# The sample's selection mask: four DMA copies on ScalarE's queue in place of two 32-row matmuls

## The chip, the cores and the metric

The kernel runs on one core of a Trainium2 chip. The metric is the device time of one execution in microseconds (us). The kernel before takes 2543.24 us, the median of three runs (2542.43 to 2546.84). TensorE is PE in the profile, VectorE is DVE, ScalarE is ACT, GpSimd is POOL, and SyncE is SP.

## What is computed

Two transformer layers run over 288 tokens: 256 prompt tokens and 32 sample tokens, which continue a stream with 512 cached positions. Each layer has one input projection, two kinds of attention side by side, an output projection and a squared-ReLU MLP (width 2048, inner width 8192), all in fp32. The part that the change touches is attention A of layer 0, in which an indexer scores every key and each query attends to its best ones only:

```python
score = jnp.einsum('bth,bths->bts', iwb.astype(F32), dots)
_, idx = lax.top_k(score, n_sel)
logits = jnp.einsum('btgrd,btkgd->btgrk', qg, k_sel) * scale
logits = jnp.where(valid[:, :, None, None, :], logits + bias, NEG_INF)
probs = jax.nn.softmax(logits, axis=-1)
```

For the 32 sample queries there are L = 544 keys (512 cached, 32 new), and 136 of them are kept per query. The kernel does not gather: it adds a mask, 0 for a chosen key and -1e30 for the others, to the bias and so to the logits.

## The kernel before

**The weight stream.** Nearly all the time goes into projections. The weights come as chunks of 128x1024 fp32, four to a group of output columns. SP loads each chunk into one of four `raw` buffers. ACT rounds it to fp32r (`high`, L839), DVE subtracts to get the remainder (`low`, L1201), and PE multiplies both halves in 24 matmuls of 288 columns (L405 to L407 in the phase here). The tiles `w_high` and `w_low` have two buffers each. So ACT's `high` of chunk c + 2 waits until PE is done with chunk c, DVE's `low` waits for that `high`, and PE's chunk c + 2 waits for that `low`.

**The windows.** Attention is cut in small pieces and laid between the chunks. Window w is the gap after chunk w of the phase on PE, and each of ACT and DVE has its own list of pieces for window w, beside the `high` or `low` of chunk w + 2. Each engine runs its list strictly in order. Attention A runs in `phase_beside`, next to the 48 chunks of B's input projection. Its 8 prompt jobs (one per head) start in windows 23 to 30. The two sample jobs, n = 8 and n = 9 (four heads each), start in windows 43 and 45. A sample tile has 128 partitions: four groups of 32, one for each head, and each group holds the 32 queries.

**The mask.** DVE finds the sample queries' top keys in rounds and breaks ties (`pick_ties`) in windows 39 to 41. The result is a tile of ones and zeros on 32 partitions, `score_s` (32x544), and DVE signals `A_chosen`. In window 42 (`W_SPREAD`) PE copies these 32 rows into all four partition groups by a product with a 32x128 matrix of stacked identities, `rep` (L696, L697). DVE turns ones and zeros in PSUM into 0 and -1e30 (L1590) and writes them to `sel_s` (128x544, SBUF). Then POOL adds `sel_s` to the bias tile of job 8 and of job 9 (L1797), each signalling `A_addend`.

**The sample job behind it.** In window 43 PE makes the scores of job 8 (L573, L574); DVE waits for `A_addend`, adds it (L1416) and takes the row maximum (L1424). In window 44 ACT takes the exponential (L965), DVE normalizes (L1434, L1440), and PE transposes the probabilities (`turn`, L590, L591). Before its `high` of window 42, ACT has stored a norm in DRAM (L925), and after it ACT issues a DMA that spreads that norm over 128 partitions (`spread_norm`, L933, into `proj`).

The lines around the mask:

```python
W_TIES_S = W_PICK_S[-1] + 1      # 39
W_SPREAD = W_TIES_S + 3          # 42
```

Of the kernel before, what the change touches and what calls it, by code (L numbers as in the profile page):

```python
# [7 lines left out]
ALU = mybir.AluOpType  # L8
# [6 lines left out]
P = 128  # L15
D = 2048
KT = D // P
TP, TS = 256, 32
T = TP + TS
L = 512 + TS  # L20
PAST = 512
H = 8
# [7 lines left out]
NEG = -1e30  # L30
# [71 lines left out]
W_SPREAD = W_TIES_S + 3  # L102
# [35 lines left out]
def build(nc, ins, outs):  # L138
    with ExitStack() as ctx:
        def sb(name, shape, dt=F32):  # L140
            return ctx.enter_context(nc.sbuf_tensor(name, shape, dt))
# [3 lines left out]
        def sem(name):  # L145
            if name not in sems:
                sems[name] = ctx.enter_context(nc.semaphore(name))
            return sems[name]
# [23 lines left out]
        ident = sb("ident", [P, P])  # L172
        ones = sb("ones", [P, P])
        fold = sb("fold", [P, TS])
        rep = sb("rep", [TS, P])
        gains = sb("gains", [P, 4, KT])
        qk_gain = sb("qk_gain", [P, 6])
        fbias = sb("fbias", [P, 1])
# [17 lines left out]
        flat = ps[:, :, :].rearrange("p b n -> p (b n)")  # L196
# [29 lines left out]
        def s3(at, a, b):  # L226
            return scr[:, at:at + a * b].rearrange("p (a b) -> p a b", a=a)
# [39 lines left out]
        score_s, work_s, equal_s = scr[0:TS, 7808:8352], scr[0:TS, 8352:8896], scr[0:TS, 7168:7168 + L]  # L267
        sel, sel_s = s3(8896, 2, TP), scr[:, 9408:9408 + L]
# [33 lines left out]
        squared, hid_high_ready, hid_low_ready = sem("squared"), sem("hid_high_ready"), sem("hid_low_ready")  # L302
# [3 lines left out]
        low_sums, summed = sem("low_sums"), sem("summed")  # L306
        consts = sem("consts")
        const_set = sem("const_set")
        NCONST = 5


        hid_at = {"A": 0, "B": JOBS, "mlp0": 2 * JOBS, "C": 2 * JOBS + 32, "D": 3 * JOBS + 32, "mlp1": 4 * JOBS + 32}
# [35 lines left out]
        def _(pe):  # L348
# [185 lines left out]
            def prelude(ph, w):  # L534
                for h in v_heads_at(ph, w):
                    turn_v(ph, h)
                for q in quads_at(ph, w):
                    norm_sums(*q)
# [148 lines left out]
                                         relu[u][:, L // 4 * c:L // 4 * (c + 1)], start=u == 0, stop=u == 1)  # L687
                last.then_inc(sem("A_scores_s"), 1)

            def spread():  # L690

                pe.wait_ge(sem("A_chosen"), 1)
                pe.wait_ge(sem("A_pt_copied"), H)
                pe.wait_ge(hid_low_ready, hid_at["A"] + H)
                pe.wait_ge(sem("B_v_copied"), H)
                pe.matmul(flat[:, 3072:3072 + PAST], rep[:, :], score_s[:, 0:PAST], start=True, stop=True)  # L696
                pe.matmul(flat[:, 3072 + PAST:3072 + L], rep[:, :], score_s[:, PAST:L], start=True, stop=True)\  # L697
                  .then_inc(sem("A_spread"), 1)

            def window_a(w):  # L700
                attend("A", w)
                prelude("A", w)
                early("B", w)
                if w == 0:
                    turn_iw()
                if w == W_DOTS_S:
                    sample_dots()
                if w == W_FOLD:
                    fold_heads()
                if W_DOTS <= w < W_DOTS + 8:  # L710
                    dots(w - W_DOTS)
                if w == W_LF + 2:
                    turn_cum()
                if w == W_SPREAD:
                    spread()

            def window_b(w):
                prelude("B", w)
# [94 lines left out]
            group(G_SMALL, G_SMALL % 2, X, tiles=1, rows=SMALL, apart=True)  # L813
            pe.wait_ge(consts, 16 * NCONST)
            phase_beside(G_INB, 0, window_a, WINDOWS["A"])
# [11 lines left out]
        def _(act):  # L827
# [115 lines left out]
            def prelude(ph, w):  # L943
                for q in quads_at(ph, w, -1):
                    squares(*q)
                for q in quads_at(ph, w, 1):
                    spread_norm(*q)
                for h in v_heads_at(ph, w):
                    copy_v(ph, h)
                for q in quads_at(ph, w):  # L950
                    rsqrt(*q)
# [93 lines left out]

            def window_a(w):
                prelude("A", w)
                if W_DOTS <= w < W_DOTS + 8:
                    dots_relu(w - W_DOTS)
                if W_DOTS_S <= w < W_DOTS_S + 2:  # L1050
                    sample_relu(w - W_DOTS_S)
                if w == W_LF - 1:
                    forget()
                attend("A", w)
                early("B", w)
# [92 lines left out]
            low_copy(2, 0)  # L1148
            act.dma_start(ident[:, :], ins["c_ident"]).then_inc(consts, 16)
            act.dma_start(fold[:, :], ins["c_fold"]).then_inc(consts, 16)  # L1150
            act.dma_start(rep[:, :], ins["c_rep"]).then_inc(consts, 16)
            act.dma_start(qk_gain[:, :], ins["qk_gain"]).then_inc(consts, 16)
            act.dma_start(fbias[ROWS, :], ins["fbias"]).then_inc(consts, 16)
            for n in range(3, IN_A):
# [33 lines left out]
        def _(dve):  # L1188
# [355 lines left out]
            def window_a(w):  # L1544
                prelude("A", w)
                if w == 0:
                    copy_iw()
                if W_DOTS_S <= w < W_DOTS_S + 2:
                    weigh_sample(w - W_DOTS_S)
                if w == W_FOLD:  # L1550
                    dve.wait_ge(sem("A_scores_s"), 1)
                    for c in range(4):
                        last = dve.tensor_copy(score_s[:, L // 4 * c:L // 4 * (c + 1)], ps[32 * c:32 * c + 32, 6, 0:L // 4])
                    last.then_inc(sem("A_score_copied"), 1)
                    dve.wait_ge(sem("A_score_copied"), 1)
                if W_DOTS <= w < W_DOTS + 8:
                    weigh_dots(w - W_DOTS)
                if w == W_LF - 1:
                    add_fbias()
                if w == W_LF:  # L1560
                    log_forget()
                if w == W_LF + 1:
                    run_cum()
                if w == W_LF + 2:
                    copy_cum()
                attend("A", w)
                if W_PICK <= w < W_TIES:
                    for i in range(2):
                        pick_round(i, score[:, i, :], work[:, i, :], P, w - W_PICK, ROUNDS_P)
                if W_TIES <= w < W_TIES + 2:  # L1570
                    i = w - W_TIES
                    chosen = sel[:, 1 - i, :]
                    for step in range(3):
                        ins_ = pick_ties(i, score[:, i, :], work[:, i, :], chosen, relu[1][:, 0:TP], P, TOP_P,
                                         chosen, step)
                    link(ins_)

                    dve.tensor_scalar(chosen, chosen, -1.0, -NEG, ALU.add, ALU.mult)\
                       .then_inc(sem("A_sel_p"), 1)
                for r in range(ROUNDS_S):  # L1580
                    if W_PICK_S[r] == w:
                        pick_round(2, score_s, work_s, TS, r, ROUNDS_S)
                if W_TIES_S <= w < W_TIES_S + 3:
                    ins_ = pick_ties(2, score_s, work_s, sel_s[0:TS, :], equal_s, TS, TOP_S, score_s,
                                     w - W_TIES_S)
                    if ins_ is not None:
                        ins_.then_inc(sem("A_chosen"), 1)
                if w == W_SPREAD:
                    dve.wait_ge(sem("A_spread"), 1)
                    dve.tensor_scalar(sel_s, flat[:, 3072:3072 + L], -1.0, -NEG, ALU.add, ALU.mult)\  # L1590
                       .then_inc(sem("A_sel_s"), 1)

            def window_b(w):
                attend("B", w)
# [112 lines left out]
            dve.wait_ge(sem("A_ik_set"), 1)  # L1707
            dve.wait_ge(consts, 16 * NCONST)

# [36 lines left out]
        def _(pool):  # L1746
            chain = [0]

            def link(ins_):
                chain[0] += 1  # L1750
                ins_.then_inc(sem("pool_chain"), 1)
                pool.wait_ge(sem("pool_chain"), chain[0])
# [29 lines left out]
            def masked(ph, n):  # L1782
                pool.wait_ge(sem(f"{ph}_bias{n % 2}"), 16 * (n // 2 + 1) + (48 if ph == "B" and n >= H else 0))
                a = addend[n % 2][:, 0:WIDE] if n < H else addend[n % 2][:, 0:L]
                if ph == "A":
                    m = sel.rearrange("p i s -> p (i s)")[:, 0:WIDE] if n < H else sel_s
                    if n == 0:
                        pool.wait_ge(sem("A_sel_p"), 2)
                    if n == H:
                        pool.wait_ge(sem("A_sel_s"), 1)  # L1790
                else:
                    if n == 0:
                        pool.wait_ge(sem("B_masks"), 32)
                    m = mask_b if n < H else mask_bs
                if ph == "B":
                    a, m = (a[:, P:WIDE], m[:, P:WIDE]) if n < H else (a[:, PAST:L], m)
                pool.tensor_tensor(a, a, m, ALU.add).then_inc(sem(ph + "_addend"), 1)  # L1797
# [244 lines left out]
```

## Time and profile before

| | us |
|---|---|
| median of three runs | 2543.24 |
| lowest and highest run | 2542.43, 2546.84 |
| the profiled execution | 2542.57 |
| its span | 2540.8 |
| PE busy | 2525.8 (99% of the span) |
| DVE busy | 1391.2 (55%) |
| ACT busy | 1006.8 (40%) |
| POOL busy | 62.7 (2%) |

A busy share counts the time in which an instruction runs on the engine. For PE the share is high because matmuls are pipelined and each lasts longer than the step to the next one; so the steps between starts tell more than durations. Times in the timeline are us from the span's start.

### The profile page before, as it was taken

How to read it: one execution, taken by the hardware profiler on the slowest of the kernel's cores; microseconds unless marked ns; L12 is line 12 of the kernel's file. 1: busy time of each engine (PE TensorE's matmuls, PEld its weight loads, DVE VectorE, ACT ScalarE, POOL GpSimd, SP SyncE). 2: the span in 40 equal slices, each digit the busy share in tenths (PEclk: the TensorE clock that was granted, in tenths of full speed). 3: DMA queues.
4: the chain of work that ended last, by engine and by line, in shares of the span. 5: the costliest groups of instructions: out<-in, count | busy, mean ns of one | idle time of the engine just before them, and what ended most of it. 6: DMA issues, size and time to landing. Idle time of an engine off the chain costs nothing.

```text
span 2540.8 us, 46922 instructions
## 1 busy us (share of the span) xinstructions
PE 2525.8 (99%) x19222; PEld 2492.8 (98%) x19222; DVE 1391.2 (55%) x1646; ACT 1006.8 (40%) x1277; POOL 62.7 (2%) x104
## 2 busy tenths in 40 slices
PE   9999999999999999999999999999999999999999
PEld 9989999999999999999999999999999999999999
DVE  5588776554554454455544564666545544544544
ACT  5344445333333333334433444454333333333332
POOL 0002120000000000000000000000000000000000
PEclk9999999999999999999999999999999999999999
DMA  6545555444444444444444545554444444444454
GB/s 232 182 163 174 197 201 206 164 166 165 166 167 166 166 165 166 167 166 165 162 166 167 180 164 201 199 180 161 166 166 166 166 166 166 166 166 166 166 180 148
DMA packets 118673, 439.20 MB, mean 173 GB/s; under 512 B 14194, under 2 KB 14452, under 8 KB 116180
## 3 DMA queue, kind: packets, MB, share of 16 engines
q1 hardware_dynamic: 109584, 398.47, 45.4%
q0 software_dynamic: 6304, 30.98, 3.4%
q10 hardware_dynamic: 2596, 6.97, 0.8%
q8 instruction: 151, 2.47, 0.4%
q14 instruction: 38, 0.31, 0.0%
HBM read 426.10 MB, written 10.19 MB: 172 GB/s over the span
## 4 chain that ended last, share of the span: by engine, by line
PE 96%; DVE 2%; ACT 1%; issue 1%; DMA 0%; POOL 0%; ACTq 0%; DVEq 0%; POOLq 0%
PE ps L405 28%; PE ps L407 28%; PE ps L406 28%; PE ps L372 2%; PE ps L374 2%; PE ps L373 2%; DVE w_low L1201 1%; PE ps L607 1%; ACT w_high L839 0%; PE ps L559 0%; PE ps L433 0%; PE ps L435 0%; PE ps L434 0%; DMA resid<-in_x 0%; PE ps L608 0%
## 5 line engine op out<-in xcount | busy, mean ns | idle before, releaser
L1201 DVE TENSOR_TENSOR w_low<-raw,w_high 128x1024 fp32r<-128x1024 f32 x755 | 921.5, 1220 | 938.0 <-ACT w_high L839 936.5
L839 ACT CAST w_high<-raw 128x1024 fp32r<-128x1024 f32 x755 | 789.7, 1046 | 1389.8 <-PE ps L407 1302.3
L405 PE MATMUL ps<-x_parts,w_high 128*128 128x288 f32 x3408 | 1013.9, 298 | 3.2 <-DVE w_low L1201 2.8
L406 PE MATMUL ps<-x_parts,w_high 128*128 128x288 f32 x3408 | 1002.5, 294 | 0.0
L407 PE MATMUL ps<-x_parts,w_low 128*128 128x288 f32 x3408 | 1001.1, 294 | 0.0
L405 PEld LDWEIGHTS ps<-x_parts,w_high 128*128 128x128 f32 x3408 | 638.1, 187 | 11.1 <-issue 7.4
L406 PEld LDWEIGHTS ps<-x_parts,w_high 128*128 128x128 f32 x3408 | 643.4, 189 | 0.2
L407 PEld LDWEIGHTS ps<-x_parts,w_low 128*128 128x128 f32 x3408 | 642.5, 189 | 0.0
L405 PE MATMUL ps<-hid_parts_a,w_high 128*128 128x288 f32 x1024 | 302.3, 295 | 0.0
L406 PE MATMUL ps<-hid_low_b,w_high 128*128 128x288 f32 x1024 | 302.3, 295 | 0.0
L407 PE MATMUL ps<-hid_high_b,w_low 128*128 128x288 f32 x1024 | 302.3, 295 | 0.0
L405 PE MATMUL ps<-hid_high_b,w_high 128*128 128x288 f32 x1024 | 301.3, 294 | 0.0
L406 PE MATMUL ps<-hid_parts_a,w_high 128*128 128x288 f32 x1024 | 301.1, 294 | 0.0
L407 PE MATMUL ps<-hid_parts_a,w_low 128*128 128x288 f32 x1024 | 300.7, 294 | 0.0
L406 PEld LDWEIGHTS ps<-hid_parts_a,w_high 128*128 128x128 f32 x1024 | 193.5, 189 | 0.0
L407 PEld LDWEIGHTS ps<-hid_parts_a,w_low 128*128 128x128 f32 x1024 | 193.3, 189 | 0.0
L406 PEld LDWEIGHTS ps<-hid_low_b,w_high 128*128 128x128 f32 x1024 | 192.4, 188 | 0.0
L407 PEld LDWEIGHTS ps<-hid_high_b,w_low 128*128 128x128 f32 x1024 | 192.3, 188 | 0.0
L405 PEld LDWEIGHTS ps<-hid_high_b,w_high 128*128 128x128 f32 x1024 | 192.1, 188 | 0.0
L405 PEld LDWEIGHTS ps<-hid_parts_a,w_high 128*128 128x128 f32 x1024 | 191.9, 187 | 0.0
L1280 DVE TENSOR_TENSOR resid<-resid,ps 128x576 f32<-128x576 f32 x64 | 48.3, 754 | 55.9 <-PE ps L407 55.9
L372 PE MATMUL ps<-hid_parts_a,w_high 128*128 128x288 f32 x256 | 78.2, 305 | 0.0
(323 smaller groups left out, 1802.8 us busy)
## 6 DMA issues: line engine op xcount, KB each, us to landing
raw<-in_w SPq DMA_DIRECT2D x755, 512.0 KB, 3.3
tmp<-norm_rows ACTq DMA_DIRECT2D x6, 576.0 KB, 4.3
proj<-norm_rows ACTq DMA_DIRECT2D x4, 576.0 KB, 4.8
scr<-in_k_past_B POOLq DMA_DIRECT2D x2, 1024.0 KB, 5.7
scr<-in_v_past_B POOLq DMA_DIRECT2D x2, 1024.0 KB, 7.3
scr<-in_k_past_C POOLq DMA_DIRECT2D x2, 1024.0 KB, 6.5
scr<-in_v_past_C POOLq DMA_DIRECT2D x2, 1024.0 KB, 7.5
scr<-in_k_past_D POOLq DMA_DIRECT2D x2, 1024.0 KB, 6.5
```

What stands on the lines that cost most here:

```text
L372: pe.matmul(out, wh, high, start=k % 8 == 0, stop=False)
L373: pe.matmul(out, wh, low, start=False, stop=False)
L374: last = pe.matmul(out, w_low[:, c % 2, at:at + P], high, start=False, stop=k % 8 == 7)
L405: pe.matmul(out, wh, high, start=k == 0, stop=end and apart)
L406: pe.matmul(out_low, wh, low, start=k == 0 and apart, stop=False)
L407: last = pe.matmul(out_low, w_low[:, kk % 2, at:at + rows], high, start=False, stop=end)
L607: pe.matmul(ps[:, 7, 0:TP], v[:, 0, :], w[:, 0:TP], start=True, stop=False)
L839: act.copy(used(n, w_high[:, kk % 2, :]), used(n, raw[:, kk, :])).then_inc(high_ready, 1)
L1201: dve.tensor_tensor(used(n, w_low[:, kk % 2, :]), used(n, raw[:, kk, :]), used(n, w_high[:, kk % 2, :]).bitcast(F32), ALU.subtract)\
L1280: dve.tensor_tensor(r, r, ps[:, 2 * odd:2 * odd + 2, 0:T], ALU.add).then_inc(evacuated, 1)
```

## The change

PE's two matmuls and the constant `rep` are taken out, with the DMA that loaded it. DVE's conversion to 0 and -1e30 moves ahead of the spreading: it is done in place on the 32 rows, in window 41, and signals `A_chosen`. In window 42 ACT waits for `A_chosen` and issues four DMAs, each of which copies the 32 rows (68 KB) to one group of 32 partitions of `sel_s`. POOL waits until all four have landed (4 x 16 = 64).

```diff
-        rep = sb("rep", [TS, P])
...
-        NCONST = 5
+        NCONST = 4
...
-            def spread():
-
-                pe.wait_ge(sem("A_chosen"), 1)
-                pe.wait_ge(sem("A_pt_copied"), H)
-                pe.wait_ge(hid_low_ready, hid_at["A"] + H)
-                pe.wait_ge(sem("B_v_copied"), H)
-                pe.matmul(flat[:, 3072:3072 + PAST], rep[:, :], score_s[:, 0:PAST], start=True, stop=True)
-                pe.matmul(flat[:, 3072 + PAST:3072 + L], rep[:, :], score_s[:, PAST:L], start=True, stop=True)\
-                  .then_inc(sem("A_spread"), 1)
...
-                if w == W_SPREAD:
-                    spread()
...
             def window_a(w):
                 prelude("A", w)
+                if w == W_SPREAD:
+                    act.wait_ge(sem("A_chosen"), 1)
+                    for j in range(4):
+                        act.dma_start(sel_s[32 * j:32 * j + 32, :], score_s).then_inc(sem("A_sel_s"), 16)
...
-            act.dma_start(rep[:, :], ins["c_rep"]).then_inc(consts, 16)
...
                     if ins_ is not None:
-                        ins_.then_inc(sem("A_chosen"), 1)
-                if w == W_SPREAD:
-                    dve.wait_ge(sem("A_spread"), 1)
-                    dve.tensor_scalar(sel_s, flat[:, 3072:3072 + L], -1.0, -NEG, ALU.add, ALU.mult)\
-                       .then_inc(sem("A_sel_s"), 1)
+                        link(ins_)
+                        dve.tensor_scalar(score_s, score_s, -1.0, -NEG, ALU.add, ALU.mult).then_inc(sem("A_chosen"), 1)
...
                     if n == H:
-                        pool.wait_ge(sem("A_sel_s"), 1)
+                        pool.wait_ge(sem("A_sel_s"), 64)
```

On PE, at the end of chunk 42 of the phase (`ps` is PSUM, `x_parts` the activations, `scr` here `score_s`), the order before:

```order
L405 MATMUL ps<-x_parts,w_high 128x288
L406 MATMUL ps<-x_parts,w_high 128x288
L407 MATMUL ps<-x_parts,w_low 128x288
L696 MATMUL ps<-scr,rep 128x512 [waits hid_low_ready,B_v_copied,A_pt_copied,A_chosen]
L697 MATMUL ps<-scr,rep 128x32
L405 MATMUL ps<-x_parts,w_high 128x288 [waits low_ready]
```

and of the change, in which these lines are numbered one lower:

```order
L404 MATMUL ps<-x_parts,w_high 128x288
L405 MATMUL ps<-x_parts,w_high 128x288
L406 MATMUL ps<-x_parts,w_low 128x288
L404 MATMUL ps<-x_parts,w_high 128x288 [waits low_ready]
L405 MATMUL ps<-x_parts,w_high 128x288
```

Chunk 43 now follows chunk 42 directly, and PE has no wait for `A_chosen` any more.

On DVE, from the last step of the ties to the logits of job 8 (`scr` is `score_s` or `sel_s`, `tmp` the probabilities' tile, `acc` the masked bias), the order before:

```order
L1485 SCALAR_TENSOR_TENSOR scr<-scr,need 32x544
L1486 TENSOR_TENSOR scr<-scr 32x544 [waits dve_chain]
L1201 TENSOR_TENSOR w_low<-raw,w_high 128x1024 [waits chunk_used,high_ready]
L1590 TENSOR_SCALAR scr<-ps 128x544 [waits A_spread]
L1337 TENSOR_TENSOR proj<-ps,rinv 128x576 [waits chunk_used]
L1201 TENSOR_TENSOR w_low<-raw,w_high 128x1024 [waits chunk_used,high_ready]
L1416 TENSOR_TENSOR tmp<-ps,acc 128x544 [waits B_normed,A_addend,A_turned,A_scored]
L1424 TENSOR_REDUCE nmax<-tmp 128x1 [waits A_s_read]
```

and of the change:

```order
L1475 SCALAR_TENSOR_TENSOR scr<-scr,need 32x544
L1476 TENSOR_TENSOR scr<-scr 32x544 [waits dve_chain]
L1578 TENSOR_SCALAR scr<-scr 32x544 [waits dve_chain]
L1191 TENSOR_TENSOR w_low<-raw,w_high 128x1024 [waits chunk_used,high_ready]
L1327 TENSOR_TENSOR proj<-ps,rinv 128x576 [waits chunk_used]
L1191 TENSOR_TENSOR w_low<-raw,w_high 128x1024 [waits chunk_used,high_ready]
L1406 TENSOR_TENSOR tmp<-ps,acc 128x544 [waits B_normed,A_addend,A_turned,A_scored]
L1414 TENSOR_REDUCE nmax<-tmp 128x1 [waits A_s_read]
```

The conversion has moved ahead of one `low` and works on 32 partitions of SBUF instead of 128 of PSUM. Ahead of the logits stand the same two instructions as before, the evacuation of a bank and a `low`.

## Rows read from the trace of the kernel before

**Rows 1.** The page: busy time, and the engines of the chain that ended last.

```profile
PE 2525.8 (99%) x19222; PEld 2492.8 (98%) x19222; DVE 1391.2 (55%) x1646; ACT 1006.8 (40%) x1277; POOL 62.7 (2%) x104
...
PE 96%; DVE 2%; ACT 1%; issue 1%; DMA 0%; POOL 0%; ACTq 0%; DVEq 0%; POOLq 0%
```

**Rows 2.** PE's waits, whole span: waiter, who ended it, us, times, longest.

```profile
PE ps L607 <- DVE scr L1644: 3.0, 1, 3.0
...
PE ps L590 <- DVE tmp L1440: 1.0, 1, 1.0
```

**Rows 3.** Timeline of PE: start, us, engine, line, operation [idle before].

```profile
292.27 0.30 PE L406 MATMUL ps<-x_parts,w_high 128*128 128x288 f32 x1
292.41 0.29 PE L407 MATMUL ps<-x_parts,w_low 128*128 128x288 f32 x1
292.65 1.12 PE L696 MATMUL ps<-scr,rep 32*128 32x512 f32 x2
...
293.84 0.40 PE L405 MATMUL ps<-x_parts,w_high 128*128 128x288 f32 x1
...
297.24 1.09 PE L573 MATMUL ps<-scr,proj 128*32 128x512 f32 x8
...
302.75 0.66 PE L590 MATMUL ps<-ident,tmp 128*128 128x128 f32 x4 [1.00 <-DVE tmp L1440]
```

**Rows 4.** Timeline of DVE, 286 to 303 us.

```profile
286.71 0.49 DVE L1481 TENSOR_SCALAR scr<-scr,top 32x544 f32<-32x544 f32 x1
...
291.88 0.71 DVE L1486 TENSOR_TENSOR scr<-scr 32x544 f32<-32x544 f32 x1
293.87 1.23 DVE L1201 TENSOR_TENSOR w_low<-raw,w_high 128x1024 fp32r<-128x1024 f32 x1 [1.28 <-ACT w_high L839]
295.01 0.72 DVE L1590 TENSOR_SCALAR scr<-ps 128x544 f32<-128x544 f32 x1
297.34 0.76 DVE L1337 TENSOR_TENSOR proj<-ps,rinv 128x576 f32<-128x576 f32 x1 [1.61 <-PE ps L407]
298.48 1.23 DVE L1201 TENSOR_TENSOR w_low<-raw,w_high 128x1024 fp32r<-128x1024 f32 x1 [0.38 <-ACT w_high L839]
299.62 0.72 DVE L1416 TENSOR_TENSOR tmp<-ps,acc 128x544 f32<-128x544 f32 x1
```

**Rows 5.** Timeline of POOL: the two additions of the mask.

```profile
295.91 2.67 POOL L1797 TENSOR_TENSOR acc<-acc,scr 128x544 f32<-128x544 f32 x2 [9.25 <-DVE scr L1590]
```

**Rows 6.** Timeline of ACT and its DMA queue (ACTq), 292 to 303 us.

```profile
292.80 1.04 ACT L839 CAST w_high<-raw 128x1024 fp32r<-128x1024 f32 x1 [2.07 <-PE ps L407]
292.87 0.32 ACTq L933 DMA_DIRECT2D proj<-norm_rows  x1
297.40 1.05 ACT L839 CAST w_high<-raw 128x1024 fp32r<-128x1024 f32 x1 [3.56 <-PE ps L407]
301.12 0.75 ACT L965 ACTIVATE tmp<-tmp,nmax 128x544 f32<-128x544 f32 x1 [2.68 <-DVE nmax L1424]
```

**Rows 7.** Timeline of ACT's queue at 50 us: issues of the constants.

```profile
50.00 1.31 ACTq L1150 DMA_DIRECT2D fold<-in_c_fold  x1
...
51.34 0.45 ACTq L1151 DMA_DIRECT2D rep<-in_c_rep  x1
```

**Rows 8.** DMA issues in 290 to 294 us: KB each, us to landing.

```profile
proj<-norm_rows ACTq DMA_DIRECT2D x1, 576.0 KB, 4.9
```

**Rows 9.** DMA queues (q1 is SP's, q10 is ACT's): packets, MB, busy share; 294.8 to 295.8, then 296.8 to 297.4 us.

```profile
q10 hardware_dynamic: 74, 0.33, 90.9%
...
q1 hardware_dynamic: 56, 0.23, 92.8%
q10 hardware_dynamic: 7, 0.02, 7.7%
```

**Rows 10.** Landing times by line: L1842 (SBUF to SBUF), then all eleven of L933.

```profile
DMA to landing us min/median/max: 2.1/2.1/2.1
...
DMA to landing us min/median/max: 3.6/4.4/7.0
```

More of the change, by code:

```diff
@@ L2000 @@
         "c_fold": fold,
-        "c_rep": fold.T,
         "mask_b": halves(causal)[:, 0:WIDE],
```

## The prediction

> **What bounds the kernel now.** I read the page first. PE is busy for 99% of the span, and 96% of the chain that ended last is PE [rows 1]. Then PE's waits: the largest of them is 3.0 us in a span of 2540.8 [rows 2]. So this kernel is a queue of matmuls, and a change can only take out matmul time, or add or take away a PE wait. One of the few PE waits there are, 1.00 us in front of L590, stands close behind the place that the change touches. So the question is not whether the matmuls cost something but what happens to that wait.
>
> The timeline shows how the two hang together. PE's last matmul of chunk 42 starts at 292.41, and neighbours start 0.13 to 0.14 us apart [rows 3]. Without the spread, chunk 43 would start at 292.54; it starts at 293.84. Behind chunk 43 comes L573 at 297.24. From there a relay runs off PE: ACT's `high` at 297.40 [rows 6], DVE's `low` at 298.48, then, without a gap, the logits of job 8 at 299.62 [rows 4]; then the maximum, ACT's exponential at 301.12 [rows 6], and PE's L590 at 302.75, for which PE has waited 1.00 us [rows 3]. From the start of the logits to L590 it is 3.13 us, and nothing in it depends on the change. The logits also need POOL's first addition of the mask. The two additions take 2.67 us from 295.91 [rows 5], so 1.34 us each, and the first was done at 297.25, 2.37 us before DVE came to the logits. That is the slack the mask has now.
>
> **What the change takes out.** PE: the spread costs 293.84 - 292.54 = 1.30 us of PE's own time, including a short wait for the end of the ties (L1486 ends at 292.59 [rows 4]). PE is the bound here, so all of it comes forward: chunk 43 ends 1.30 us earlier, and ACT's `high` and DVE's `low` go with it, since both wait for PE [rows 4, 6]. The `low` that chunk 44 needs ends at 295.10 [rows 4], before chunk 43 would end at about 295.9, so PE does not run into it. DVE: L1590 (0.72 us) goes, and a 32x544 operation comes in. L1481 is the same kind on the same shape, 0.49 us [rows 4]. Both stand in idle time of DVE: after L1486 it waits 1.28 us for ACT [rows 4], and the new one ends at about 292.6 + 0.5 = 293.1. I count 0 for DVE; if that cover were gone, the cost would be 0.5 us. The load of `rep`: one issue of 0.45 us on ACT's queue at 51 us [rows 7], where no PE wait lies near; 0.
>
> **What it adds.** Four DMA issues on ACT, behind a wait for `A_chosen`. In ACT's list they stand behind L933, which is issued at 292.87 and takes 0.32 us [rows 6], so ACT is there at 293.19, about when `A_chosen` comes. No row shows this copy. The nearest issue is that of `rep`, also 32 partitions: 0.45 us [rows 7]. Then the four begin at about 293.2, 293.6, 294.1 and 294.5 and end at 295.0. Behind them on ACT is the `high` for which PE gives the word at about 296.1 (297.40 - 1.30). So the wait and the issues lie in ACT's idle 3.56 us [rows 6] and cost 0.
>
> The price is the time until all four have landed. The lower bound is the nearest copy from SBUF to SBUF, 2.1 us from issue [rows 10]: 294.5 + 2.1 = 296.6. The upper bound is the slowest DMA of ACT's queue that this trace has, 7.0 us [rows 10]: 301.5. Which of the two is nearer? Just ahead on the same queue lies the 576 KB of L933, which lands after 4.9 us, at 297.8 [rows 8]. The queue's data is still moving at 295 us, and hardly at 297 us [rows 9]. From 296 us on SP's queue with the next 512 KB of weights has the engines, at 93% at 297 us [rows 9]. I take it that the copies' data starts only when L933's is through, at about 296.9. They are 4 x 68 = 272 KB and share the engines about evenly with the weights. At 0.23 MB in 0.6 us [rows 9], some 0.38 MB/us in all, the 0.28 MB are done when twice as much has moved, 1.5 us later, at 298.4. L933's landing at 297.8 came 0.4 us behind the last stretch in which its queue moved anything to speak of. I estimate the mask at 298.4 + 0.4 = 298.8.
>
> One rule of the Trainium skill says this much: its page "DMA: Bandwidth & Descriptors", section "Queues, rings and completion order", has each engine take one ring's descriptors in order and go round-robin between queues. By that rule the copies queue behind L933 and share with SP. The trace agrees so far that L933's data and the weights run side by side, but it has no copy behind L933.
>
> **The sum.** POOL starts 0.18 us after its release (295.73 to 295.91 [rows 4, 5]), adds for 1.34, and I give the way to DVE another 0.1 to 0.2: 1.7 us from landing to logits. 298.8 + 1.7 = 300.5. Without the mask DVE would be ready at 299.62 - 1.30 = 298.3. So the logits wait 2.2 us for the mask, and L590 comes at 300.5 + 3.13 = 303.6 instead of 302.75: 0.9 us later than now. What PE gained in window 42 goes into its wait at L590, which grows from 1.0 to about 3.2 us. Nothing else is late: ACT's next `high`, behind that exponential, and the `low` on it also come 0.9 us later, but for a chunk ahead of which PE still has a whole other one to do (3.4 us, from 293.84 to 297.24 [rows 3]). Job 9's mask is ready 1.3 us after job 8's, and its logits come two windows later. The change costs **+0.9 us**. The profiled execution would go from 2542.57 to 2543.5, and the median, which stands 0.67 above that execution, from 2543.24 to **2544.1 us**.
>
> By the mask's landing, the sum turns at two points. Up to 296.6 the whole 1.3 us is kept. At 297.9 (299.62 - 1.7) it is zero. After that each us late costs one. The bounds give -1.3 us (landing at 296.6) and +3.6 us (301.5).
>
> **Rivals.**
> *A, the mask is in time.* The copies don't queue behind L933, or start while its data is running, and land at 296.6 to 297.4. Then the logits start at 298.3 to 299.1 and the time is 2543.24 - 1.3 to - 0.5, about 2542.3. For it: the SBUF copy at 2.1 us [rows 10]. Against it: engines that are over 90% busy at 295 and 297 us [rows 9]. The skill's fit for one DMA (same page, section "Anatomy of one DMA") of 2.0 us plus bytes over 436 GB/s, though given for the other issuing path, would put 68 KB at 2.16 us, so at 296.7, and this rival would come true. The eleven landings of L933, none under 3.6 us at 576 KB, neither show it nor exclude it.
> *B, the issues themselves are slow.* Place: ACT's queue in window 42. The constant `fold` took 1.31 us to issue, where L933 took 0.32 [rows 6, 7]. If each of the four takes that, the last starts at 293.2 + 3 x 1.31 = 297.1 and ACT is free only at 298.4, 2.3 us after PE's word for `high`. Landing at 297.1 + 2.1 to 4.9 gives 299.2 to 302.0 and +1.3 to +4.1 us: 2544.5 to 2547.3, slower by at most 0.16%. It decides from an issue time of about 0.7 us on. Against it: `rep`, of the copies' number of partitions, took 0.45, and it was itself issued behind others.
> *C, no gain at the matmuls.* The change removes the spread, but the 1.30 us come back at once as another PE wait in chunks 43 to 44, with the mask in time: 2543.2, no change. Only the `low` ending at 295.10 could do that, and it has 0.8 us to spare.
>
> **How the numbers follow.** My forecast (landing at 297.6 to 300, so -0.3 to +2.1 us) gets 0.60, A 0.22, B and landings later than 300 us 0.13, C 0.05. The bounds of all are -1.3 and +4.1 us, so 2541.9 to 2547.3. The runs before lie 0.8 below to 3.6 above their median, and a new median of few runs can move by a part of that; I take 2541.4 to 2547.2, which leaves out 2 in 10 at most.
>
> A measurement of this kernel tells 0.2%, about 5.1 us, from no change. No case reaches it: the largest gain is 1.3 us, the largest loss 4.1 us. Only something the rows don't show could (a change of code or addresses that moves waits elsewhere; a copy that lands some 6 us late). I give faster 0.02, same 0.94, slower 0.04, a little more on the slow side since the wait has no upper limit.
>
> **What the profile after would show.** Right: L696 and L697 gone, and chunk 43 starting about 0.13 us behind the last matmul of chunk 42; four issues on ACT's queue of about 0.45 us each; landing of the last about 4 us after its issue; the first mask addition on POOL released by a DMA at about 299; DVE's logits of job 8 released by POOL at about 300.5; PE's wait ahead of the transposes at about 3.2 us instead of 1.0; ACT's `high` still released by PE. Wrong: POOL starting before 297 us (A), ACT's queue busy beyond 296 us (B), or a new wait of PE at chunk 44 (C). The forecast fails as a whole if the span moves by more than 5 us.

## The result: 4.7 us slower, ratio 1.0019

The change takes 2549.71 us (median of 19 runs, 2546.90 to 2552.99), the kernel before 2544.99 us in the same rounds (19 runs, 2542.43 to 2546.94). The ratio is 1.0019, with a 95% interval of 1.0012 to 1.0025: slower, and above the range of 2541.4 to 2547.2 that was given. The median of before also rose from the three runs that the prediction had (2543.24), so 1.75 us of the miss are in the base, and the rest is in the change: +4.7 us where +0.9 was forecast. One run of e6 and one of e12 below took 6362.80 and 3463.72 us and are left out of the medians.

### The profile page after: what moved, and what is told of

It reads as the page before. It is cut to its first block, busy times and chain, and to the rows that moved or that the text cites. A ratio compares the mean times of both kernels' runs of the same rounds, so it can differ in the third digit from the quotient of the medians.

```text
span 2546.7 us, 46915 instructions
## 1 busy us (share of the span) xinstructions
PE 2526.4 (99%) x19218; PEld 2494.2 (98%) x19218; DVE 1391.8 (55%) x1646; ACT 1008.9 (40%) x1277; POOL 62.9 (2%) x104
## 4 chain that ended last, share of the span: by engine, by line
PE 95%; DVE 2%; ACT 1%; issue 1%; DMA 1%; ACTq 0%; POOL 0%; DVEq 0%; POOLq 0%
PE ps L404 28%; PE ps L406 28%; PE ps L405 28%; PE ps L371 2%; PE ps L373 2%; PE ps L372 2%; DVE w_low L1191 1%; PE ps L606 1%; ACT w_high L826 0%; PE ps L558 0%; PE ps L432 0%; PE ps L434 0%; PE ps L433 0%; DMA resid<-in_x 0%; PE ps L607 0%
## 5 line engine op out<-in xcount | busy, mean ns | idle before, releaser
L1191 DVE TENSOR_TENSOR w_low<-raw,w_high 128x1024 fp32r<-128x1024 f32 x755 | 922.2, 1221 | 939.2 <-ACT w_high L826 937.8
L406 PE MATMUL ps<-hid_parts_a,w_low 128*128 128x288 f32 x1024 | 300.7, 294 | 0.0
```

The costliest lines, as they stand in the source:

```text
L406: last = pe.matmul(out_low, w_low[:, kk % 2, at:at + rows], high, start=False, stop=end)
L1191: dve.tensor_tensor(used(n, w_low[:, kk % 2, :]), used(n, raw[:, kk, :]), used(n, w_high[:, kk % 2, :]).bitcast(F32), ALU.subtract)\
```

## The profile after

In the changed kernel the lines of the matmuls that concern us carry numbers one lower, those of the other engines numbers 10 to 13 lower: L589 is the old L590, L606 the old L607, L613 the old L614, L1191 the `low`, L1406 the logits, L1784 POOL's addition, L1038 the copies. The profiled execution took 2548.46 us, its span is 2546.7 us. The page, busy time:

```profile
PE 2526.4 (99%) x19218; PEld 2494.2 (98%) x19218; DVE 1391.8 (55%) x1646; ACT 1008.9 (40%) x1277; POOL 62.9 (2%) x104
```

PE is busy 0.6 us more than before [rows 1] although two matmuls are gone, in a span 5.9 us longer. PE's waits (the view of [rows 2]):

```profile
PE ps L589 <- DVE tmp L1430: 5.1, 1, 5.1
PE ps L606 <- DVE scr L1631: 3.0, 1, 3.0
...
PE ps L432 <- DVE x_parts L1287: 2.5, 2, 2.2
```

The wait ahead of the transposes has grown from 1.0 to 5.1 us and is now the largest of the kernel. The waits of L432 lie in the first microseconds and are 1.3 us in before's profile. They scatter from run to run (1.7 to 3.8 us in the profiles below, of kernels with and without copies), and they shift all that follows. I therefore measure the stage from a point of its own: the start of ACT's `high` in window 42, 292.80 before [rows 6] and 293.90 after. Here is PE's timeline, to set beside [rows 3]:

```profile
296.92 1.08 PE L572 MATMUL ps<-scr,proj 128*32 128x512 f32 x8
...
306.54 1.12 PE L589 MATMUL ps<-ident,tmp 128*128 128x128 f32 x4 [5.07 <-DVE tmp L1430]
...
308.38 0.44 PE L404 MATMUL ps<-x_parts,w_high 128*128 128x288 f32 x1
308.62 0.44 PE L405 MATMUL ps<-x_parts,w_high 128*128 128x288 f32 x1
...
312.24 1.05 PE L613 MATMUL ps<-scr 128*128 128x128 f32 x8
```

In before's profile the same piece, the next one of attention behind the chunk, starts at 306.52:

```profile
306.52 1.05 PE L614 MATMUL ps<-scr 128*128 128x128 f32 x8
```

Three things stand here. L572 comes 3.02 us behind the `high`, before it was 4.44 (297.24 - 292.80): the matmuls' time is gained, 1.4 us. L589 comes at 12.64 instead of 9.95: 2.7 us lost. And the matmuls of the chunk behind it start 0.24 us apart instead of 0.13, so L613 is 5.70 us behind L589 where the same distance was 3.77 us (306.52 - 302.75) before: another 1.9 us. In sum the stage is 4.62 us longer (18.34 instead of 13.72). The wait grew by 4.07, the slow chunk adds 1.93, and the gain takes off 1.4, so next to nothing is left over. Of the 5.9 us between the two spans, 1.1 us lie ahead of the stage (293.90 against 292.80) and 0.2 behind it. The medians, 4.7 us apart, agree with the stage. The granted clock confirms the last part of it; busy time of the engines in a stretch, then the clock as a share of 2.4 GHz, then DMA:

```profile
306.50:310.50 4.00, 3.96 (x17) 3.90 (x18) 2.68 (x3) 0.93 (x3) 0.00 (x0) 0.50 0.33 106
310.50:314.00 3.50, 3.50 (x28) 3.08 (x30) 0.42 (x1) 1.30 (x2) 0.00 (x0) 0.97 0.09 33
```

For 4 us behind the wait TensorE ran at 0.50, its level of 1.2 GHz. In before's profile the clock is 1.00 in every stretch of 6 us.

DVE, to set beside [rows 4]:

```profile
293.74 0.43 DVE L1578 TENSOR_SCALAR scr<-scr 32x544 f32<-32x544 f32 x1
...
298.17 1.23 DVE L1191 TENSOR_TENSOR w_low<-raw,w_high 128x1024 fp32r<-128x1024 f32 x1 [0.38 <-ACT w_high L826]
303.39 0.72 DVE L1406 TENSOR_TENSOR tmp<-ps,acc 128x544 f32<-128x544 f32 x1 [4.00 <-POOL acc L1784]
```

POOL, beside [rows 5]:

```profile
301.94 2.62 POOL L1784 TENSOR_TENSOR acc<-acc,scr 128x544 f32<-128x544 f32 x2 [14.18 <-DMA scr<-scr]
```

and ACT with its queue, beside [rows 6]:

```profile
293.90 1.05 ACT L826 CAST w_high<-raw 128x1024 fp32r<-128x1024 f32 x1 [2.06 <-PE ps L406]
293.98 0.32 ACTq L920 DMA_DIRECT2D proj<-norm_rows  x1
294.35 2.54 ACTq L1038 DMA_DIRECT2D scr<-scr  x4
297.08 1.05 ACT L826 CAST w_high<-raw 128x1024 fp32r<-128x1024 f32 x1 [2.13 <-PE ps L406]
```

DVE is ready for the logits at 299.4 and stands there for 4.00 us until POOL has added the mask, and POOL waits for the copies. ACT is not held up: its next `high` is released by PE. The four issues take 0.61 us each (minimum 0.602, maximum 0.615) and the landings are, one by one, 4.2, 4.6, 4.7 and 5.5 us behind them; the line of L1038:

```profile
DMA to landing us min/median/max: 4.2/4.7/5.5
```

The last copy, issued at 296.3, is there at 301.8. What the two DMA queues moved meanwhile (q1 is SP's, q10 is ACT's; packets, MB, busy share), from 298 to 299 and from 299 to 300 us:

```profile
q10 hardware_dynamic: 83, 0.14, 48.4%
q1 hardware_dynamic: 26, 0.11, 39.4%
...
q1 hardware_dynamic: 65, 0.25, 83.5%
q10 hardware_dynamic: 25, 0.04, 14.5%
```

## The experiments

All are made from the changed kernel, but for the two with a late mask, which are made from the kernel before. Where lines shift, L582 is the filler, L589, L590 or L593 the transposes. Each group ran on one chip, with before in the same rounds. "Stage" is the distance from the `high` of window 42 to the first L613 (or L614, L617), 13.72 us before. "Behind" is its last part, from the transposes on, 3.77 us at full clock.

| run | median, us | before, us | ratio (95%) | PE's wait | behind | stage |
|---|---|---|---|---|---|---|
| the change | 2549.71 | 2544.99 | 1.0019 (1.0012 to 1.0025) | 5.07 | 5.70 | 18.34 |
| e9 the change again | 2549.76 | 2544.81 | 1.0019 (1.0010 to 1.0028) | 5.67 | 6.30 | 19.52 |
| e1 40 fillers | 2550.93 | 2544.47 | 1.0026 (1.0016 to 1.0035) | none | 3.75 | 20.08 |
| e5 18 fillers | 2548.80 | 2544.29 | 1.0018 (1.0009 to 1.0027) | 1.64 | 3.77 | 16.98 |
| e10 22 fillers | 2548.25 | 2544.81 | 1.0016 (1.0007 to 1.0024) | 1.24 | 3.77 | 17.47 |
| e2 copies ahead of the norm | 2546.68 | 2544.47 | 1.0009 (1.0000 to 1.0018) | 3.60 | 6.28 | 17.44 |
| e11 two copies | 2547.42 | 2544.81 | 1.0009 (1.0000 to 1.0018) | 3.86 | 6.34 | 17.76 |
| e4 one window earlier | 2547.28 | 2544.47 | 1.0011 (1.0002 to 1.0020) | 2.41 | 5.30 | see text |
| e6 before, mask 3 additions late | 2547.57 | 2544.29 | 1.0012 (1.0003 to 1.0021) | 3.17 | 5.32 | 17.44 |
| e7 before, mask 5 additions late | 2551.27 | 2544.29 | 1.0026 (1.0016 to 1.0036) | 5.46 | 5.29 | 19.72 |
| e3 DVE writes the mask | 2544.96 | 2544.47 | 1.0004 (0.9995 to 1.0013) | 1.98 | 3.81 | 13.35 |
| e8 the same, additions apart | 2542.87 | 2544.29 | 0.9995 (0.9986 to 1.0004) | 0.97 | 3.81 | 12.34 |
| e12 the same again | 2541.49 | 2544.81 | 0.9989 (0.9981 to 0.9998) | 0.97 | 3.81 | 12.35 |

### Is the slow clock a cost of its own?

PE multiplies ones by ones during its wait, into a bank that the transposes overwrite:

```diff
             def turn(ph, n):
 
+                if ph == "A" and n == H:
+                    pe.wait_ge(sem("A_pt_copied"), n)
+                    for _ in range(40):
+                        pe.matmul(ps[:, 6, 0:P], ones[:, :], ones[:, :], start=True, stop=True)
                 pe.wait_ge(sem(ph + ("_probs" if n < H or ph == "A" else "_exps")), n + 1)
```

> The change as it is, with 40 matmuls of 128x128 (0.11 us each, into the bank that the transposes of job 8 overwrite) issued by PE while it waits for the probabilities of job 8. Theory (two costs: a later mask, about 2.7 us of wait beyond what the removed matmuls give back, and then about 1.9 us because the granted clock falls to the lower level behind the 5.07 us wait): the wait stays, L589 and the chunk behind it run at the step of 0.13 us, and the stage from the end of chunk 42 to L613 is 1.9 us shorter than in the change; time about 2547.8. Rival (the clock has another cause, or the slow matmuls cost nothing since ACT and DVE hold the chunks anyway): the same time as the change, 2549.7.

This run missed its size. A filler is two passes of 0.11 us, so the 40 ran for 9 us, past the end of the wait:

```profile
302.91 9.09 PE L582 MATMUL ps<-ones 128*128 128x128 f32 x80
```

Its time of 2550.93 us says nothing on the clock's price. But the chunk behind ran at full clock (3.75 us). With 18, and later 22:

> The change with 18 filler matmuls instead of the 40 of the earlier run, which ran 9 us and so 3.3 us past the probabilities they were to wait for (each is 0.22 us in two passes). 18 take 4.0 us and fit into the wait of 5.07. Theory (the clock falls behind the wait and costs 1.9 us on top of it): L589 starts at the same distance from the end of the ties as in the change, the chunk behind it runs at 0.13 us per matmul, time 1.9 us below the change, 2547.8. Rival (a falling clock costs nothing, the chunk waits for its low anyway): as the change, 2549.7.

> The change with 22 filler matmuls, 4.9 us, nearly the whole wait. The version with 18 left 1.64 us of wait, ran its chunk at full clock in the profile, and yet its median was 4.5 us above before. Theory (clock loss is 1.9 us and more in part of the runs): median 1.5 to 2.5 us below the change in this group. Rival (the fillers take away the slow clock in the trace but not the time, which would then come from something else): within 0.7 us of the change in this group.

> The change itself once more, on the chip and in the rounds of the three others of this group, so that the filler's effect is read against it and not against before. Expected: about 4.7 us above before, a wait of about 5 us ahead of the transposes, and slow clock behind it.

The timeline of the run with 18:

```profile
300.40 4.18 PE L582 MATMUL ps<-ones 128*128 128x128 f32 x36
306.22 0.66 PE L593 MATMUL ps<-ident,tmp 128*128 128x128 f32 x4 [1.64 <-DVE tmp L1434]
...
309.99 1.05 PE L617 MATMUL ps<-scr 128*128 128x128 f32 x8
```

From the transposes to the next piece it is 3.77 us again, as before, against 5.70 and 6.30 in the two profiles of the change. So the slow clock is a cost of its own, of 1.9 and 2.5 us in these two, and work on PE during the wait takes it away. The medians point the same way but don't show it: 22 fillers are 1.5 us faster than the change in the same rounds (2548.25 against 2549.76), at the low end of what was expected, and the two sets of eleven runs overlap (2547.53 to 2551.30 and 2547.07 to 2553.17). 18 gave a median only 0.2 us nearer to before, far from the 1.9 us of its theory. Part of the difference is that in both filler profiles the mask landed later than in the change (POOL at 8.6 and 9.1 us behind the `high`, 8.0 and 8.6 in the change's two). The trace settles the mechanism; the medians alone would not have.

### Is it the lateness of the mask, or the copies as such?

The kernel before, matmuls and all, with extra additions of the mask to itself on POOL (0 stays 0), and no copy:

```diff
                     if n == H:
                         pool.wait_ge(sem("A_sel_s"), 1)
+                        for _ in range(3):
+                            link(pool.tensor_tensor(m, m, m, ALU.add))
```

> The kernel before, matmul spread and all, with three extra additions of the mask to itself on POOL (0 stays 0, -1e30 gets larger) ahead of job 8's, about 4.2 us in all: no copy at all, only a mask that comes late. The slack is 2.37 us, so the logits come 1.9 us later and PE's wait is about 2.9 us. Theory (lateness alone makes the loss, and the clock falls behind a wait of this length as it did behind 2.41 us): +1.9 us and 1.5 to 2.5 us of slow clock, time about 3.9 us above before. Rival (the clock falls only because of the copies or at a longer wait): +1.9 us.

> As the run with three extra additions, with five, about 7.0 us in all. The logits come 4.6 us later than before and PE's wait is about 5.6 us. Theory: +4.6 and about 2 us of slow clock, 6.5 us above before. Rival (clock without price): +4.6.

PE's waits in the first and in the second:

```profile
PE ps L590 <- DVE tmp L1440: 3.2, 1, 3.2
```

```profile
PE ps L590 <- DVE tmp L1440: 5.5, 1, 5.5
```

The waits came near what was computed (3.17 and 5.46 us, 2.9 and 5.6 expected), and the clock fell behind both; in the run with five the 303 to 315 us stretch was granted 0.72, the same as in the change. The stage grew by 3.72 and 6.00 us: 2.2 and 4.5 us by the wait, 1.5 us each by the slow chunk. The medians rose by 3.3 and 7.0 us. The theory held in the traces; the medians alone, with intervals that reach down to 1.0003 and 1.0016, would still admit the rival (clock without price). A mask that is late without any DMA makes the same kind of loss as the change, and the change's own stage adds up without another term. So no harm of the copies beyond their landing time is seen.

### Why does the mask land so late?

```diff
             def window_a(w):
-                prelude("A", w)
                 if w == W_SPREAD:
                     act.wait_ge(sem("A_chosen"), 1)
                     for j in range(4):
                         act.dma_start(sel_s[32 * j:32 * j + 32, :], score_s).then_inc(sem("A_sel_s"), 16)
+                prelude("A", w)
```

> The change with the four copies issued ahead of the spreading of the norm in window 42, not behind it. Theory (the copies wait in ACT's ring behind 576 KB): the last lands some 2.5 to 3 us after its issue instead of 5.5, the addition on POOL starts 2.5 us earlier, PE's wait is about 2.5 us and the clock stays up: time 2549.7 - 2.5 - 1.9 = 2545.3. Rival (the engines are simply full with weights, the order in ACT's queue is nothing): landing 5 us or more after issue, time as the change.

The landing line of the copies:

```profile
DMA to landing us min/median/max: 2.1/2.5/4.2
```

One by one they took 2.5, 2.5, 2.1 and 4.2 us. The same copies behind the 576 KB of the norm had taken 4.2 to 5.5. This fits a queue that is served in order, in which the 576 KB ahead cost the first three about 2 us each. The last one is different: in the stretch from 297 to 298 us SP's weights held the engines at 95.2% and ACT's queue moved nothing:

```profile
q1 hardware_dynamic: 95, 0.39, 95.2%
```

It was waiting then, and landed at 299.2. That the weights delayed it is read from this line; no run took them away. The wait was 3.60 us instead of the 2.5 expected, and the clock fell in the profiled run (behind: 6.28 us), against my expectation. The median is 2546.68 us, where 2545.3 was expected, and the eleven runs spread widely, 2542.91 to 2550.86 us. The rule of the Trainium skill that the prediction weighed ("DMA: Bandwidth & Descriptors", section "Queues, rings and completion order": one ring is served in order, queues take turns) agrees with these landings in its first half. The second half is not seen in the stretch above, where a copy was pending and its queue moved nothing.

With only two copies, DVE writing the other two groups:

```diff
-                    for j in range(4):
+                    for j in (2, 3):
                         act.dma_start(sel_s[32 * j:32 * j + 32, :], score_s).then_inc(sem("A_sel_s"), 16)
...
                         link(ins_)
+                        for j in range(2):
+                            last = dve.tensor_scalar(sel_s[32 * j:32 * j + 32, :], score_s, -1.0, -NEG, ALU.add, ALU.mult)
+                        link(last)
                         dve.tensor_scalar(score_s, score_s, -1.0, -NEG, ALU.add, ALU.mult).then_inc(sem("A_chosen"), 1)
...
-                        pool.wait_ge(sem("A_sel_s"), 64)
+                        pool.wait_ge(sem("A_sel_s"), 32)
```

> DVE writes the mask to the first two groups of partitions, and only two copies are issued. A_chosen comes 0.9 us later, the last issue starts 0.3 us earlier than with four. Theory (the landing is set by the queue ahead and the weights, so half the copies help little beyond their own bytes): last landing at 4.5 to 5 us from its issue, PE's wait 3.5 to 4.5 us, clock falls, about 1 us below the change. Rival (issue time and bytes of the copies themselves set it): landing within 3.5 us, wait under 3 us.

The two landed 4.0 and 4.8 us behind their issue, PE waited 3.86 us, and the median was 2.3 us below the change's in the same rounds, where about 1 us was expected. The landings and the wait are near those of the theory: half the copies still take 4.0 us and more. But fewer copies are worth something, for POOL started 6.80 us behind the `high`, 8.62 in the change in the same rounds.

### Everything one window earlier

```diff
-W_PICK_S = [5, 6, 7, 8, 9, 10, 11, 31, 32, 33, 34, 35, 36, 37, 37, 38, 38]
+W_PICK_S = [5, 6, 7, 8, 9, 10, 11, 31, 32, 33, 34, 35, 35, 36, 36, 37, 37]
```

> The change with the last rounds of the pick packed tighter, so that ties, mask and copies all come one window (3 to 4 us) earlier, and the copies stand ahead of the spreading of the norm, which stays in window 42. Theory: the mask lands about 4 us earlier or more, ahead of the logits; PE's wait back to about 1.0 us, no clock loss, time 1.3 us below before, if DVE carries two rounds per window without being late with a low. Rival (DVE becomes late in windows 35 to 38): new PE waits for low there, time above before.

This failed, at a place I had not expected. ACT and its queue:

```profile
292.05 0.50 ACTq L912 DMA_DIRECT2D norm_rows<-rs  x1
292.59 2.52 ACTq L1038 DMA_DIRECT2D scr<-scr  x4
295.22 1.05 ACT L826 CAST w_high<-raw 128x1024 fp32r<-128x1024 f32 x1 [3.20 <-issue]
```

In window 41 the issues stand behind the rooting and storing of the norm (L912), not behind a wait. `A_chosen` was there at 291.4 and the first issue came at 292.59. The four issues then held the `high` behind them until 295.22; PE had to wait 1.0 us more for a `low`. The `high` being moved, the norm's root (L907, the old L920) is the mark here: L589 came 13.01 us behind it, 13.00 before (302.75 - 289.75). So the mask was not late at all compared with before, and PE's time ahead of it was only turned into a wait of 2.41 us. But the clock fell even behind that wait, and the next 3.77 us became 5.30. The median is 2.8 us above before. My statement that issuing costs nothing on ACT held in window 42, where 3.56 us were free [rows 6], and not one window earlier.

This run also limits what was said of the queue. Here the 576 KB stood behind the copies, and ahead of them only the store of the norm (4.5 KB). Still they landed 4.3, 4.1, 4.6 and 4.7 us behind their issues. From 294 to 295 us, with all of them issued or being issued, ACT's queue moved nothing, and SP's weights held the engines at only 33.9%:

```profile
q1 hardware_dynamic: 33, 0.13, 33.9%
```

So the 576 KB are one reason for a late landing and not the only one; what held these copies stays open.

### What are the removed matmuls worth?

No matmul and no copy; DVE writes the four groups itself:

```diff
-                if w == W_SPREAD:
-                    act.wait_ge(sem("A_chosen"), 1)
-                    for j in range(4):
-                        act.dma_start(sel_s[32 * j:32 * j + 32, :], score_s).then_inc(sem("A_sel_s"), 16)
...
                         link(ins_)
-                        dve.tensor_scalar(score_s, score_s, -1.0, -NEG, ALU.add, ALU.mult).then_inc(sem("A_chosen"), 1)
+                        for j in range(4):
+                            last = dve.tensor_scalar(sel_s[32 * j:32 * j + 32, :], score_s, -1.0, -NEG, ALU.add, ALU.mult)
+                        last.then_inc(sem("A_sel_s"), 1)
...
-                        pool.wait_ge(sem("A_sel_s"), 64)
+                        pool.wait_ge(sem("A_sel_s"), 1)
```

> No matmul and no DMA: DVE writes the mask itself into the four groups of partitions with four 32x544 operations in window 41. Theory (the removed matmuls are worth 1.3 us if the mask is in time): DVE busy 1.7 us more in idle time, mask ready near 295.5 plus the offset of that run, PE's wait before the transposes 1.0 us as before, time 1.3 us below before. Rival (the 1.3 us come back as a wait elsewhere, or DVE's 1.7 us delay the low of the next chunk): time as before or above.

The four took 1.78 us and fitted. But only 0.37 us of the stage was left of the gain, and PE's wait was 1.98 us instead of 1.0. DVE and POOL:

```profile
294.56 1.22 DVE L1187 TENSOR_TENSOR w_low<-raw,w_high 128x1024 fp32r<-128x1024 f32 x1
...
297.17 2.23 DVE L1187 TENSOR_TENSOR w_low<-raw,w_high 128x1024 fp32r<-128x1024 f32 x1 [0.38 <-ACT w_high L826]
```

```profile
294.70 3.62 POOL L1782 TENSOR_TENSOR acc<-acc,scr 128x544 f32<-128x544 f32 x2 [7.93 <-DVE scr L1575]
```

The `low` ahead of the logits took 2.23 us instead of 1.23, and POOL's two additions 3.62 us instead of 2.67 [rows 5]. If POOL's second addition is the cause, holding it back must cure it (this line comes on top of the version above):

```diff
             masked("A", H)
+            pool.wait_ge(sem("A_s_read"), H + 1)
             masked("A", H + 1)
```

> The version in which DVE writes the mask to all four groups, with POOL's addition for job 9 held back until the logits of job 8 have been read. Theory (in the version without this the low before the logits took 2.23 us instead of 1.23 since it ran beside POOL's second addition, and that ate 1.0 of the 1.3 us gained): the low is 1.23 us again, PE's wait 1.0, time 1.3 us below before. Rival (the low was slow for another reason): 2.2 us again, and the time as before.

> The version without copies and without matmuls, with POOL's second addition held back, once more for more runs: 1.3 us below before by its trace, so a ratio near 0.9995. Rival: a chance result, ratio at 1.000.

```profile
294.75 2.30 POOL L1782 TENSOR_TENSOR acc<-acc,scr 128x544 f32<-128x544 f32 x1 [7.92 <-DVE scr L1575]
299.15 1.36 POOL L1782 TENSOR_TENSOR acc<-acc,scr 128x544 f32<-128x544 f32 x1 [2.10 <-DVE tmp L1402]
```

```profile
297.21 1.23 DVE L1187 TENSOR_TENSOR w_low<-raw,w_high 128x1024 fp32r<-128x1024 f32 x1 [0.38 <-ACT w_high L826]
```

The `low` is 1.23 us again, the wait 0.97, and the stage 12.34 us: 1.38 below before, where 1.3 was expected. The repetition gave 12.35 us and a ratio of 0.9989 (0.9981 to 0.9998); in the first group the interval (0.9986 to 1.0004) still held no change. By the stage in both profiles, and by the medians of the second group (2541.49 against 2544.81 us), this version is faster than both kernels. It does what the change wanted, to take the matmuls out, with no transfer.

### The same slow clock, in the kernel before

Why do equal kernels scatter by 5 us? The 3.0 us wait at L607 (L606 behind the change) [rows 2] stands at about 1520 us, far from the mask, and is 2.99 to 3.02 us in all fourteen profiles. The first line is from before's profile, the second from that of e9:

```profile
1521.20 0.70 PE L607 MATMUL ps<-scr 128*128 128x256 f32 x2 [3.02 <-DVE scr L1644]
...
1526.85 1.22 PE L606 MATMUL ps<-scr 128*128 128x256 f32 x2 [2.99 <-DVE scr L1631]
```

In before, the change and e7 the clock stayed at 1.00 behind it, and it is 7.10 to 7.13 us to the next transposes (L801 or its like). In the eleven others it fell to 0.50, and the same distance is 8.60 to 9.93 us: 1.5 to 2.8 us lost. So before's own profile had luck here, and so had the change's. The 97 runs of before in the three groups of experiments fall in two heaps: 21 with a mean clock of 1.000 take 2542.33 to 2543.25 us, 76 with 0.999 take 2543.84 to 2547.18. No run of the second heap was profiled, so that it is this wait that parts them is likely and not shown. It is also why the stages above tell more than the medians.

## Why the prediction was wrong

**What held.** PE is the bound, and the place to look is the wait ahead of the transposes. The removal is worth 1.30 us: 1.38 in e8, where nothing took it back. The four issues don't hold ACT's `high` in the change. DVE's new operation lies in idle time (0.43 us, 0.49 assumed). POOL is released by the DMA and DVE by POOL, and 1.6 us passed from landing to logits, 1.7 assumed. Rivals A (mask in time) and C (another wait at once) did not come. B had its issues too dear: 0.61 us, below the 0.7 from which it would decide.

**The first step that failed is the landing.** It was put at 298.8 us in before's time and was 301.8 - 1.10 = 300.7, so 1.9 us later. The order was right: the copies' data followed the 576 KB and ran beside weights. The term that was mis-sized is the time for the copies' own data, 1.5 us at an even share of 0.38 MB/us. Neither the rate nor the even share held. The two queues together moved 0.24 to 0.29 MB/us from 298 to 301 us, and from 299 to 301 us the weights moved 0.45 MB and ACT's queue 0.08. The issues were mis-sized too, 0.61 us and not 0.45, which puts the last of them at 295.2 instead of 294.5. By the prediction's own reasoning that costs nothing, as both lie ahead of 296.9, when the 576 KB were to be through; no run tests that by itself. With 0.1 us less from landing to logits the wait became 5.07 instead of 3.2 us, and L589 came 2.7 us late instead of 0.9. A landing behind 300 us had been thought of, together with B, at 0.13.

**The second step that failed was missing from the sum.** "The change costs +0.9 us" ended at the transposes; behind them the text took PE's pace as given. It wasn't: the chunk behind the wait ran at 1.2 GHz, 1.9 us in the change's profile and 2.5 us in the second. That is as much as the misjudged landing, and it can come even at the 3.2 us that I forecast: e6 has a wait of 3.17 us and pays 1.5 us behind it, e4 has 2.41 us and pays the same. With it my own sum would have been +2.4 us or more. The trace of before could not show the price, since its clock is 1.00 throughout, and its waits of up to 3.0 us [rows 2] are followed by none of it. Most other runs of before do show a lower mean clock. The range's upper end, +4.1 us, had no place for it either.

**The certainty was too great.** "No case reaches 0.2%" rested on a list of cases without the clock. The result, 0.19%, lies at that bound.

## What to carry to other kernels

A step that is moved off the bounding engine onto a transfer must be priced with its landing behind all that stands ahead in its queue and beside what other queues move, and compared with the slack of whoever waits; here 1.3 us of matmul were given for a wait that grew by 4.1 us. When TensorE is the bound, a new wait of a few microseconds can cost more than its length, because the work behind it may run at half clock; filling the wait with harmless matmuls took that part away in two profiles, and no wait is better still. Look first for an engine with idle time that can write the result in place: four 0.44 us operations on DVE did what four DMAs could not.

## What the runs showed of the hardware

**The clock behind a wait.** At the transposes TensorE fell to 0.50 of its clock behind waits of 2.41, 3.17, 3.60, 3.86, 5.07, 5.46 and 5.67 us, and not behind 0.97, 1.00, 1.24, 1.64 and 1.98 us. The price was not proportional: 1.5 us behind the wait of 5.46, 2.5 behind that of 3.60 or 3.86. Length alone is not the whole rule. At one other place a wait of 3.0 us was followed by the slow clock in eleven profiles and not in three, and at 12 us one of 2.20 us was in e1 (clock 0.64 and then 0.51) and one of 2.2 to 2.3 us was not in the change or e12; the runs don't say what decides. The fall need not come before PE resumes: behind 2.41 and 3.17 us the first four transposes still took 0.66 us as before, behind 5.07 us 1.12. The page "TensorE: Matmul & The Clock Gate" of the Trainium skill, section "HAM oscillation — how this bites in real kernels", describes such falls in a loop whose matmuls wait for a DMA in every round; here a single wait was enough. The 30 runs of the change take 2546.90 to 2549.30 us where their mean granted clock is 0.999 and 2550.97 to 2553.17 where it is 0.997.

**VectorE and GpSimd in each other's way.** A `tensor_tensor` of DVE with both inputs in SBUF took 2.23 us beside an addition on POOL and 1.23 without; POOL's addition took 2.30 us where a `low` ran beside it and 1.36 where none did. In e6 and e7 the `low` in the same place took 1.95 and 1.97 us. The page "SBUF — State Buffer", section "Who interferes with whom", says that a DVE instruction with two SBUF inputs contends with a GpSimd instruction that reads SBUF, and that the ports they share are locked exclusively. The runs agree: in e3 and e8 each delay is about 1 us, most of the other's duration.

**Four copies from the same 32 partitions.** The first three in e2 landed 2.1 to 2.5 us behind their issue, and no others came under 3.6 us. They cost 0.61 us per issue on ACT's queue, where a DMA from DRAM to 128 partitions issues in 0.32 us and one to 32 partitions in 0.45 [rows 6, 7].
